# Ten RMS norms of a fused three-block kernel: sums put with tokens on partitions, the root taken on two columns, the result spread by TensorE

## The chip, the cores and the metric

The kernel runs on one NeuronCore of one Trainium2 chip. The metric is the device time of one execution in microseconds (us), taken as the median of several runs. A profiled execution beside them gives a trace of every instruction on the core: TensorE (PE, with its weight loads as PEld), VectorE (DVE), ScalarE (ACT), GpSimd (POOL), and the queue of SyncE (SP), which here issues all DMAs.

## What is computed

A batch of one, 256 tokens, width 1024, all float32. First a two-layer block (each layer: SwiGLU FFN, a mixer, SwiGLU FFN; the mixers are MLA and RWKV-7), then a second block (a Hyena and HGRN mixer, then 16 experts, each taking its 32 best tokens). Every stage begins with the same norm, modulated by vectors that come from a condition c:

```python
def _rmsnorm(x, g):
    y = x * rsqrt(mean(x * x, axis=-1, keepdims=True) + EPS)
    return y * g

def _modulate(x, g, shift, scale):
    return _rmsnorm(x, g) * (1 + scale) + shift

for i in range(2):
    mods = (silu(c) @ ada_w[i] + ada_b[i]).reshape(B, 3, 3, D_MODEL)
    h = _modulate(x, norm_g[i, 0], mods[:, 0, 0], mods[:, 0, 1])
    x = x + 0.5 * mods[:, 0, 2] * _swiglu(h, ffn_w_in[i, 0], ffn_w_out[i, 0])
    h = _modulate(x, norm_g[i, 1], mods[:, 1, 0], mods[:, 1, 1])
    x = x + mods[:, 1, 2] * mixer(h)          # MLA for i = 0, RWKV-7 for i = 1
    h = _modulate(x, norm_g[i, 2], mods[:, 2, 0], mods[:, 2, 1])
    x = x + 0.5 * mods[:, 2, 2] * _swiglu(h, ffn_w_in[i, 1], ffn_w_out[i, 1])
x = _rmsnorm(x, final_g)
# second block: norm, w_in, Hyena + HGRN, w_out, norm, router and experts, final norm
```

## The kernel before

Activations are held transposed: `x3` (tile `xT`) and `h3` (in `hT_sq`) have the 1024 features on partitions, as 8 tiles of 128 features (kt or m = 0 to 7), and the 256 tokens along the free dimension. Weights come from DRAM as slots of 1 or 2 MB. Each engine has its instruction stream written out by hand, in program order, and the engines meet at semaphores. There is no scheduler.

**A norm, before.** Norms are numbered 0 to 9. Norm 0 stands at the launch, norm 1 ahead of MLA, 2 and 3 ahead of FFNs 1 and 2, 4 ahead of RWKV, 5 ahead of FFN 3, 6 is the last norm of the first block, 7 and 8 are the first of the second block (of x, and of a context), 9 stands ahead of the router. ScalarE squares x in four steps of two tiles (L1386) into `sq3`. TensorE multiplies a 128x128 matrix of ones (the stationary operand) with each squared tile (256 columns, L664), so that PSUM bank 7 holds the sum of squares of each token, repeated on all 128 partitions. VectorE scales it and adds epsilon (L1728, 128x256), ScalarE takes the root (L1374, 128x256), VectorE the reciprocal (L1724, 128x256), all in the tile `rstd`. Then VectorE makes eight tiles of h, each `x * scale * rstd` (L1731), and ScalarE adds the shift to each (L1391), and TensorE's next stage waits for each of the eight in turn (`h_part`).

After the sums TensorE issues some matmuls on zeros (`keep_clock`, L659, bf16, 512 columns) whose result nobody reads. The number of them stands in the call: `norm(2, 10)` is norm 2 with 10 of them.

**The launch, before.** SP issues silu's input `c_rows`, one slot of the modulation weights (`ada`), then x, `vec` and a part of `con` (the `start_landed` loads), then two `ada` slots, the first FFN's gate and up slots, five `ada` slots, and the down slot. Then come four `ada` slots, each after a wait for a dot product of VectorE (`ada_used`), and the next gate slot once TensorE is done with the first. VectorE takes dot products of the `ada` slots with silu(c) (`first_dots`, L1757, two for each slot q = 0 to 7); slot q gives scale and shift for tile q of x. VectorE takes q = 0 and 1 ahead of norm 0 and q = 2 to 7 behind it. GpSimd multiplies x with `rstd` (L1688). ScalarE makes h (L1402 to L1408) when the dots and GpSimd's tile are there, and `first_group` on TensorE (L722) takes the eight tiles of h one by one.

**Between norm 6 and the second block.** TensorE computes the spectra of two filters, `filter_freq(0)` and `filter_freq(1)` (L1039 to L1043). The second may begin when VectorE has emptied the PSUM banks of the first (`filter_end(0)`, whose last instruction is L2083). Norm 7's sums stand between the two. In VectorE's stream norm 7's root and reciprocal follow `filter_end(0)`. Norm 8's sums stand between two units of `b2_in` (L1071), a chain of products of 7 us each, and its result is wanted three units later.

**The end.** The experts read 192 slots of 2 MB (`expert_load`, L597) into nine places of SBUF, each refilled when TensorE has used it. The ninth is issued behind the transposition of h after norm 9, and the tenth when TensorE has used the first.

## Time and profile before

| | us |
|---|---|
| median of 3 runs | 2678.49 |
| lowest, highest | 2677.92, 2680.62 |
| the profiled execution | 2676.36 |
| its span in the trace | 2674.30 |
| PE busy | 2302.1 (86%) |
| DVE busy | 774.6 (29%) |
| ACT busy | 344.9 (13%) |
| DMA queue q1 | 707.79 MB, 65.6% of 16 engines |

The span is what lies between the first and the last instruction; 2.06 us of the profiled execution lie around it. The busy shares are means over stages of different kinds: up to some 1750 us TensorE is the busy engine, after it the DMA engines are.

### The profile page before, as it was taken

Reading aid. Unit: us, or ns where it says so; the run is one execution under the profiler, and the core shown is the slowest. Engines: PE = TensorE matmul, PEld = TensorE weight load, DVE = VectorE, ACT = ScalarE, POOL = GpSimd, SP = SyncE. Lnnn points to the kernel's source line nnn. Section 1 sums busy time; section 2 is a strip of 40 time slices with the busy share of each in tenths; the row PEclk is TensorE's granted clock in tenths of the full one; section 3 lists DMA queues with packets and bytes.
Section 4 is the critical chain, followed back from the end, with each engine's and each line's share of the span. In section 5 each row is a group of like instructions: output and inputs, shape, how many; then the busy total and the mean of one; then the engine's idle time right before and its main releaser. Section 6 shows DMA issues by size and latency. Waiting matters only on the chain.

```text
span 2674.3 us, 34093 instructions
## 1 busy us (share of the span) xinstructions
PE 2302.1 (86%) x14956; PEld 1619.0 (61%) x14968; DVE 774.6 (29%) x1473; ACT 344.9 (13%) x618; POOL 17.5 (1%) x21
## 2 busy tenths in 40 slices
PE   7999989999999999999999999896666666666675
PEld 5888768888888789888886878652121111111221
DVE  5544534574000465511023338640000000000000
ACT  3001222002000232111002211210000000000000
POOL 1000000000000000000000000000000000000000
PEclk9999999999999999999999999988887788887778
DMA  9889235886445240044442223489999999999997
GB/s 394 343 354 379 95 142 226 354 341 256 157 141 204 90 147 20 24 169 148 136 172 78 66 77 115 189 330 428 428 427 428 426 428 427 428 427 427 426 428 338
DMA packets 70098, 709.51 MB, mean 265 GB/s; under 512 B 7776, under 2 KB 7904, under 8 KB 8672
## 3 DMA queue, kind: packets, MB, share of 16 engines
q1 hardware_dynamic: 69984, 707.79, 65.6%
q8 instruction: 96, 1.57, 0.2%
q14 instruction: 18, 0.15, 0.0%
HBM read 706.71 MB, written 1.05 MB: 265 GB/s over the span
## 4 chain that ended last, share of the span: by engine, by line
PE 62%; DMA 30%; DVE 7%; ACT 1%; issue 1%; SPq 0%; DVEq 0%; ACTq 0%
DMA arena<-in_experts 27%; PE ps L691 11%; PE ps L698 11%; PE ps L708 11%; PE ps L757 5%; PE ps L875 4%; PE ps L1071 4%; PE ps L1282 2%; PE ps L1314 2%; DMA ring<-in_experts 2%; PE ps L664 1%; PE ps L1069 1%; PE ps L773 1%; PE ps L1247 1%; PE ps L787 1%
## 5 line engine op out<-in xcount | busy, mean ns | idle before, releaser
L1282 PE MATMUL ps<-arena 128*32 128x512 f32 x1376 | 211.8, 748 | 147.0 <-DMA arena<-in_experts 146.5
L691 PE MATMUL ps<-hT_sq,arena 128*128 128x256 f32 x1376 | 312.1, 380 | 4.1 <-ACT hT_sq L1391 2.9
L708 PE MATMUL ps<-hid,arena 128*128 128x256 f32 x1408 | 311.1, 379 | 0.2 <-DVE hid L1796 0.2
L698 PE MATMUL ps<-hT_sq,arena 128*128 128x256 f32 x1376 | 311.0, 379 | 0.0
L708 PEld LDWEIGHTS ps<-hid,arena 128*128 128x128 f32 x1408 | 267.4, 190 | 36.9 <-issue 0.6
L691 PEld LDWEIGHTS ps<-hT_sq,arena 128*128 128x128 f32 x1376 | 260.5, 190 | 45.5 <-issue 8.5
L698 PEld LDWEIGHTS ps<-hT_sq,arena 128*128 128x128 f32 x1376 | 261.4, 190 | 35.5
L1282 PEld LDWEIGHTS ps<-arena 128*32 128x32 f32 x1376 | 42.4, 124 | 310.6 <-DMA arena<-in_experts 226.0
L1363 ACT ACTIVATE arena<-ps 128x512 f32<-128x512 f32 (+4 forms) x147 | 89.1, 615 | 946.1 <-PE ps L1293 308.5
L1796 DVE TENSOR_TENSOR hid<-sil,ps 128x256 f32<-128x256 f32 x88 | 37.0, 421 | 560.4 <-ACT sil L1415 560.2
L1757 DVE CUSTOM_DVE_ANT_0 hT_sq<-arena 128x1024 f32<-128x1024 f32 x168 | 194.5, 1221 | 0.0
L2249 DVE TENSOR_TENSOR arena<-arena,ps 128x512 f32<-128x512 f32 x16 | 11.0, 688 | 552.4 <-PE ps L1282 552.4
L1314 PE MATMUL ps<-arena 128*32 128x512 f32 x688 | 108.7, 767 | 36.5 <-DMA arena<-in_experts 33.1
L1415 ACT ACTIVATE sil<-ps 128x256 f32<-128x256 f32 x88 | 33.7, 383 | 779.3 <-PE ps L698 778.9
L1282 PE MATMUL ps<-ring,arena 128*32 128x512 f32 x512 | 79.3, 751 | 48.3 <-DMA ring<-in_experts 48.3
L757 PE MATMUL ps<-arena,ring 128*128 128x256 f32 x512 | 111.5, 379 | 2.6 <-DVE arena L1894 1.8
L757 PEld LDWEIGHTS ps<-arena,ring 128*128 128x128 f32 x512 | 97.1, 190 | 17.6 <-DVE arena L1894 2.3
L2256 DVE TENSOR_TENSOR arena<-ps,arena 128x512 f32<-128x512 f32 x16 | 11.1, 692 | 306.4 <-PE ps L1314 306.4
L875 PE MATMUL ps<-arena 64*64 64x64 f32 x2848 | 85.9, 218 | 3.0 <-ACT arena L1363 2.1
L875 PEld LDWEIGHTS ps<-arena 64*64 64x64 f32 x2848 | 84.4, 135 | 3.8 <-ACT arena L1363 2.5
L1314 PEld LDWEIGHTS ps<-arena 128*32 128x32 f32 x688 | 22.4, 128 | 105.7 <-DMA arena<-in_experts 49.0
L1071 PE MATMUL ps<-hT_sq,ring 128*128 128x256 f32 x384 | 83.9, 379 | 0.0
(370 smaller groups left out, 2184.0 us busy)
## 6 DMA issues: line engine op xcount, KB each, us to landing
arena<-in_experts SPq DMA_DIRECT2D x129, 2048.0 KB, 41.1
arena<-in_ada SPq DMA_DIRECT2D x96, 1024.0 KB, 9.7
ring<-in_experts SPq DMA_DIRECT2D x42, 2048.0 KB, 40.9
ring<-in_ring_w SPq DMA_DIRECT2D x51, 1024.0 KB, 5.1
arena<-in_ffn_gate SPq DMA_DIRECT2D x44, 1024.0 KB, 6.5
arena<-in_ffn_up SPq DMA_DIRECT2D x44, 1024.0 KB, 6.2
arena<-in_ffn_down SPq DMA_DIRECT2D x44, 1024.0 KB, 4.8
hT_sq<-in_experts SPq DMA_DIRECT2D x21, 2048.0 KB, 40.4
```

The source lines that it names most:

```text
L691: last = mm(ps[:, ft, 0:T], gate3[:, kt, ft * P:(ft + 1) * P], h3[:, kt, :], start=kt == 0, stop=kt == KT - 1)
L698: last = mm(ps[:, ft, T:2 * T], up3[:, kt, ft * P:(ft + 1) * P], h3[:, kt, :], start=kt == 0, stop=kt == KT - 1)
L708: last = mm(acc(m), down3[:, ft, m * P:(m + 1) * P], hid3[:, ft, :], start=False, stop=True, skip_group_check=True)
L757: last = mm(out_of(m), slot(seq0 + kt // 2)[:, (kt % 2) * D + m * P:(kt % 2) * D + (m + 1) * P], rhs3[:, kt, :], start=(kt == 0 and m % 2 ...
L875: last = mm(ps[r, bank, kt * HD:(kt + 1) * HD], lhs[r, kt, :], rhs[r, :] if len(rhs.shape) == 2 else rhs[r, kt, :], start=start and (stop ...
L1071: last = mm(o, w[:, kt, j * P:(j + 1) * P], src[:, kt, :], start=kt == 0, stop=kt == KT - 1)
L1282: last = mm(ps[32 * n:32 * n + 32, part, :], e_xe[:, kt, :], w[:, (kt % 2) * SLOT + n * 512:(kt % 2) * SLOT + (n + 1) * 512], start=kt == ...
L1314: last = mm(ps[q:q + 32, 3, :], e_hT[:, i, 32 * n:32 * n + 32], w[:, i * D + nn * 512:i * D + (nn + 1) * 512], start=n == 0 and i < 2, sto ...
L1363: return f(dst, src, ACT.Copy)
L1415: f(sil3[:, ft, :], ps[:, ft, 0:T], ACT.Silu).then_inc(sem("silu_ready"), 1)
L1757: nc.vector.tensor_tensor_reduce(buf[:, out_at * D:(out_at + 1) * D], w, c_rows[:, which * D:(which + 1) * D], 1.0, 0.0, ALU.mult, ALU.add ...
L1796: tt_(hid3[:, ft, :], sil3[:, ft, :], ps[:, ft, T:2 * T], ALU.mult).then_inc(sem("hid_ready"), 1)
```

## The change

- **Sums.** The squared tile becomes the stationary operand, in two halves of 128 tokens, and one column of ones the moving one: 16 matmuls of one column in place of 8 of 256. The sums of the two token halves stand in two PSUM columns, `norm_sums`, with tokens on partitions.
- **Root and reciprocal** work on 128x2 (`norm_unit`, in `small`).
- **Spreading.** `widen` multiplies each column of `norm_unit`, repeated 128 times by its access pattern as the stationary operand, with the identity: two matmuls of 128x128 into `norm_wide`, half of PSUM bank 7. VectorE reads that in place of `rstd`. In TensorE's stream `widen` stands behind 5 or 6 matmuls on zeros and waits for the reciprocal. In norm 7 it stands ahead of `filter_freq(1)`, in norm 8 behind one more unit of `b2_in`.
- **The launch.** x, `vec` and `con` are loaded first. ScalarE squares x before silu. VectorE takes only q = 0 ahead of norm 0, multiplies x with the spread root itself, and takes q = 1 to 7 behind that. GpSimd has no part in it. TensorE has 16 more matmuls on zeros ahead of the sums.

```diff
-        def norm_sums(i):
-            return ps[:, 7, 0:T]
+        norm_sums, norm_wide, norm_unit = ps[:, 7, 0:TT], ps[:, 7, T:2 * T], small[:, 240:240 + TT]
...
+            start()
             sp.dma_start(c_rows[:, 0:D], a["c_rows"][:, 0:D]).then_inc(sem("c_landed"), 16)
-            first_rows(0, 1)
-            start()
-            first_rows(1, 3)
+            first_rows(0, 3)
...
-            def norm(i, busy=0):
+            def norm(i, busy=(0, 0)):
+                if i == 7:
+                    pe.wait_ge(sem("x_ready"), 7 * KT)
                 for kt in range(KT):
                     pe.wait_ge(sem("squares"), 4 * i + kt // 2 + 1)
-                    last = mm(norm_sums(i), ones, sq3[:, kt, :], start=kt == 0, stop=kt == KT - 1)
+                    for tt in range(TT):
+                        last = mm(norm_sums[:, tt:tt + 1], sq3[:, kt, tt * P:(tt + 1) * P], ones[:, 0:1],
+                                  start=kt == 0 and tt == 0, stop=kt == KT - 1, skip_group_check=True)
                 last.then_inc(sem("norm_sum"), 1)
-                keep_clock(6, busy)
+                if busy:
+                    keep_clock(6, busy[0])
+                    widen(i)
+                    keep_clock(6, busy[1])
+
+            def widen(i):
+                pe.wait_ge(sem("norm_unit"), i + 1)
+                for tt in range(TT):
+                    last = mm(norm_wide[:, tt * P:(tt + 1) * P], norm_unit[:, tt:tt + 1].to_broadcast([P, P]), ident,
+                              start=True, stop=True)
+                last.then_inc(sem("norm_wide"), 1)
...
-                        norm(8)
+                        norm(8, None)
+                    if u == CTX_AT + 1:
+                        widen(8)
...
+            keep_clock(6, 16)
             pe.wait_ge(sem("start_landed"), 48)
-            norm(0, 12)
+            norm(0, (6, 20))
             ffn(0, 1)
-            norm(1, 20)
+            norm(1, (5, 8))
             mla()
-            norm(2, 10)
+            norm(2, (5, 2))
             ffn(1, 3)
-            norm(3, 10)
+            norm(3, (5, 2))
             ffn(2, 4)
-            norm(4, 18)
+            norm(4, (5, 9))
             rwkv()
-            norm(5, 10)
+            norm(5, (5, 2))
             ffn(3, 6)
-            norm(6, 11)
+            norm(6, (5, 5))
             filter_freq(0)
-            norm(7)
+            norm(7, None)
+            keep_clock(0, 5)
+            widen(7)
             filter_freq(1)
...
-            norm(9, 10)
+            norm(9, (5, 3))
...
-                root(rstd[:, :])
+                if i == 0:
+                    act.wait_ge(sem("c_landed"), 16)
+                    f(c_rows[:, 0:D], c_rows[:, 0:D], ACT.Silu).then_inc(sem("c_ready"), 1)
+                root(norm_unit)
...
-            act.wait_ge(sem("c_landed"), 16)
-            f(c_rows[:, 0:D], c_rows[:, 0:D], ACT.Silu).then_inc(sem("c_ready"), 1)
...
-            pool.wait_ge(sem("x_root"), 1)
-            for kt in range(KT):
-                nc.gpsimd.tensor_tensor(x_unit[:, kt, :], x3[:, kt, :], rstd[:, :], ALU.mult).then_inc(sem("x_scaled"), 1)
...
-                inverse_root(ts(rstd[:, :], norm_sums(i), 1.0 / D, EPS, ALU.mult, ALU.add), rstd[:, :])
+                root(ts(norm_unit, norm_sums, 1.0 / D, EPS, ALU.mult, ALU.add))
+                nc.vector.reciprocal(norm_unit, norm_unit).then_inc(sem("norm_unit"), 1)
+                dve.wait_ge(sem("norm_wide"), i + 1)
                 for m in range(KT):
-                    stt(out=dst[:, m, :], in0=src[:, m, :], scalar=scale[:, m:m + 1], in1=rstd[:, :], op0=ALU.mult, op1=ALU.mult) \
+                    stt(out=dst[:, m, :], in0=src[:, m, :], scalar=scale[:, m:m + 1], in1=norm_wide, op0=ALU.mult, op1=ALU.mult) \
                         .then_inc(sem(name), 1)
...
-            first_dots(0, 2)
+            first_dots(0, 1)
...
-            root(ts(rstd[:, :], norm_sums(0), 1.0 / D, EPS, ALU.mult, ALU.add))
-            nc.vector.reciprocal(rstd[:, :], rstd[:, :]).then_inc(sem("x_root"), 1)
-            first_dots(2, 2 * NADA)
+            root(ts(norm_unit, norm_sums, 1.0 / D, EPS, ALU.mult, ALU.add))
+            nc.vector.reciprocal(norm_unit, norm_unit).then_inc(sem("norm_unit"), 1)
+            dve.wait_ge(sem("norm_wide"), 1)
+            for kt in range(KT):
+                tt_(x_unit[:, kt, :], x3[:, kt, :], norm_wide, ALU.mult).then_inc(sem("x_scaled"), 1)
+            first_dots(1, 2 * NADA)
```

In the lists below a row is a run of equal instructions of one engine in program order; `x8` counts them, and a float32 matmul counts once here though the trace shows two records for it.

TensorE around norm 2, before: L664 are the sums, L659 the matmuls on zeros, L675 opens the banks of FFN 1, L691 is its first product.

```order
L757 MATMUL ps<-hT_sq,ring 128x256 x64
L664 MATMUL ps<-hT_sq,con 128x256 x8
L659 MATMUL ps<-zeros 128x512 x10
L675 MATMUL ps<-zeros 128x512 x4
L736 UNCONDITIONAL_BRANCH
L736 ISA
L691 MATMUL ps<-hT_sq,arena 128x256 x8
```

The same place after the change: L664 are the sums, L656 the matmuls on zeros, L676 is `widen`, L687 opens the banks.

```order
L769 MATMUL ps<-hT_sq,ring 128x256 x64
L664 MATMUL ps<-con,hT_sq 128x1 x16
L656 MATMUL ps<-zeros 128x512 x5
L676 MATMUL ps<-con,small 128x128 x2
L656 MATMUL ps<-zeros 128x512 x2
L687 MATMUL ps<-zeros 128x512 x4
L748 UNCONDITIONAL_BRANCH
L748 ISA
L703 MATMUL ps<-hT_sq,arena 128x256 x8
```

The ten matmuls on zeros have become five, `widen`, and two.

TensorE around norm 7, before: L664 are norm 7's sums, the first L1039 below them begins `filter_freq(1)`.

```order
L1043 MATMUL ps<-arena 128x512 x2
L664 MATMUL ps<-hT_sq,con 128x256 [waits squares] x8
L1039 MATMUL ps<-arena 128x512 [waits filter_done,filter_sides]
L1039 MATMUL ps<-arena 128x512
L1041 MATMUL ps<-arena 128x512 x2
```

The end of the sums of norm 7 and what follows, after the change: L1051 begins `filter_freq(1)`.

```order
L664 MATMUL ps<-con,hT_sq 128x1 [waits squares]
L664 MATMUL ps<-con,hT_sq 128x1
L656 MATMUL ps<-zeros 128x512 x5
L676 MATMUL ps<-con,small 128x128 [waits norm_unit]
L676 MATMUL ps<-con,small 128x128
L1051 MATMUL ps<-arena 128x512 [waits filter_done,filter_sides]
L1051 MATMUL ps<-arena 128x512
L1053 MATMUL ps<-arena 128x512 x2
```

`filter_freq(1)` now stands behind a wait for norm 7's reciprocal (`norm_unit`) as well, and behind `widen`.

VectorE at the launch, before: L1757 are the dot products of q = 1, then norm 0 (L2286, L2287), then q = 2. A row `dots 128x1` belongs to the dot product above it.

```order
L1757 ISA arena,dots<-arena 128x1024 [waits ada_first,ada_landed1]
L1757 ISA dots 128x1
L1757 ISA arena,dots<-arena 128x1024 [waits ada_used]
L1757 ISA dots 128x1
L2283 SCALAR_TENSOR_TENSOR coef<-vec 128x8 [waits start_landed]
L2286 TENSOR_SCALAR rstd<-ps 128x256 [waits norm_sum]
L2287 RECIPROCAL rstd<-rstd 128x256 [waits root_out]
L1757 ISA arena,dots<-arena 128x1024 [waits ada_first,ada_landed2]
```

The same place after the change: norm 0 is L2302 and L2303, the eight multiplications of x are L2306, and q = 1 follows.

```order
L1773 ISA arena,dots<-arena 128x1024
L1773 ISA dots 128x1
L2299 SCALAR_TENSOR_TENSOR coef<-vec 128x8 [waits start_landed]
L2302 TENSOR_SCALAR small<-ps 128x2 [waits norm_sum]
L2303 RECIPROCAL small<-small 128x2 [waits root_out]
L2306 TENSOR_TENSOR arena<-xT,ps 128x256 [waits norm_wide]
L2306 TENSOR_TENSOR arena<-xT,ps 128x256 x7
L1773 ISA arena,dots<-arena 128x1024 [waits ada_first,ada_landed1]
```

The dot products of q = 1 to 7 now stand behind the multiplications of x.

## Rows read from the trace of the kernel before

**Rows 1.** Page: DMA share in 40 slices (tenths); the chain by engine

```profile
DMA  9889235886445240044442223489999999999997
...
PE 62%; DMA 30%; DVE 7%; ACT 1%; issue 1%; SPq 0%; DVEq 0%; ACTq 0%
```

**Rows 2.** Timeline, norm 2: start us, us, engine, line, operation [idle before <-releaser]

```profile
403.67 3.62 PE L664 MATMUL ps<-hT_sq,con 128*128 128x256 f32 x16
...
404.79 0.63 ACT L1386 ACTIVATE hT_sq<-xT 128x512 f32<-128x512 f32 x1 [0.24 <-DVE xT L1752]
...
407.34 2.10 PE L659 MATMUL ps<-zeros 128*128 128x512 bf16 x9
407.40 0.42 DVE L1728 TENSOR_SCALAR rstd<-ps 128x256 f32<-128x256 f32 x1 [2.58 <-PE ps L664]
407.86 0.42 ACT L1374 ACTIVATE rstd<-rstd 128x256 f32<-128x256 f32 x1 [1.14 <-DVE rstd L1728]
408.31 1.75 DVE L1724 RECIPROCAL rstd<-rstd 128x256 f32<-128x256 f32 x1 [0.48 <-ACT rstd L1374]
...
410.10 3.25 DVE L1731 SCALAR_TENSOR_TENSOR hT_sq<-xT,coef,rstd 128x256 f32<-128x256 f32 x8
...
411.27 3.04 PE L691 MATMUL ps<-hT_sq,arena 128*128 128x256 f32 x13 [0.95 <-ACT hT_sq L1391]
```

**Rows 3.** Timeline around 1594 us: another root and reciprocal, on 128x2

```profile
1594.84 0.20 ACT L1374 ACTIVATE small<-small 128x2 f32<-128x2 f32 x1
1595.07 0.17 DVE L1724 RECIPROCAL small<-small 128x2 f32<-128x2 f32 x1 [1.34 <-ACT small L1374]
```

**Rows 4.** Timeline of TensorE, 1745 to 1794 us: float32 matmuls, stationary 128x128

```profile
1745.23 7.03 PE L1247 MATMUL ps<-arena 128*128 128x32 f32 x32
...
1782.40 3.74 PE L1302 MATMUL ps<-con,xT 128*128 128x128 f32 x32
...
1789.64 3.76 PE L1247 MATMUL ps<-arena 128*128 128x32 f32 x32
```

**Rows 5.** Timeline: the last two dot products at launch, FFN 0's second group

```profile
36.62 0.08 DVE L1757 DVE_READ_ACCUMULATOR2_ANT dots<- 128x1 f32 x1
...
37.76 0.08 DVE L1757 DVE_READ_ACCUMULATOR2_ANT dots<- 128x1 f32 x1
...
49.84 3.72 PE L691 MATMUL ps<-hT_sq,arena 128*128 128x256 f32 x16 [1.25 <-DMA arena<-in_ffn_gate]
```

**Rows 6.** Stretches: us, PE, PEld, DVE, ACT, POOL busy, PEclk, DMA share, GB/s

```profile
20.00:36.00 16.00, 12.14 (x46) 9.85 (x47) 15.24 (x21) 6.65 (x18) 12.16 (x8) 0.89 1.01 420
36.00:50.00 14.00, 11.90 (x52) 9.22 (x51) 10.62 (x19) 5.26 (x9) 0.00 (x0) 1.00 1.02 413
```

**Rows 7.** The launch's last two `ada` slots: issues, and issue to landing

```profile
L561 SPq DMA_DIRECT2D arena<-in_ada x2: 458/612/765, 7.1 to 7.6; - x2
...
DMA to landing us min/median/max: 23.7/24.7/25.7
```

**Rows 8.** Timeline of TensorE: the first product of MLA, after norm 1

```profile
267.38 22.64 PE L773 MATMUL ps<-hT_sq,ring 128*128 128x256 f32 x96 [2.31 <-ACT hT_sq L1391]
```

**Rows 9.** Two of the slots it reads (1 and 2): issue and landing

```profile
L592 SPq DMA_DIRECT2D ring<-in_ring_w x2: 447/450/454, 241.8 to 242.3; - x2
...
DMA to landing us min/median/max: 22.9/23.8/24.8
```

**Rows 10.** Timeline of norm 7 and the begin of `filter_freq(1)`

```profile
1427.67 1.22 DVE L2083 TENSOR_TENSOR arena<-ps,arena 128x1024 f32<-128x1024 f32 x1
1428.80 0.41 DVE L1728 TENSOR_SCALAR rstd<-ps 128x256 f32<-128x256 f32 x1
...
1429.03 3.34 PE L1039 MATMUL ps<-arena 128*128 128x512 f32 x4 [4.01 <-DVE arena L2083]
```

**Rows 11.** A stretch of it, columns as in rows 6

```profile
1429.00:1432.00 3.00, 2.97 (x4) 1.42 (x5) 2.48 (x4) 0.42 (x1) 0.00 (x0) 0.53 0.02 5
```

**Rows 12.** Timeline of TensorE behind norm 8's sums

```profile
1471.63 20.88 PE L1071 MATMUL ps<-hT_sq,ring 128*128 128x256 f32 x96
```

## The prediction

> **What bounds the kernel now.** I read the page first: the chain that ended last lies on TensorE for 62% of the span and on DMA for 30%, on VectorE for 7% [rows 1]. The slices of DMA show where each holds: nearly full in the first four slices (267 us), partly full up to slice 27, full from there to the end [rows 1]. So up to some 1750 us a microsecond saved on TensorE's path ahead of a stage is a microsecond of the whole, and the experts' DMA stream behind it starts as much earlier: its tenth slot is asked for when TensorE has used the first. What it takes from then on does not depend on the norms. Two places differ: where TensorE, when a norm is done, waits for a transfer all the same, and where TensorE does not wait for the norm at all. So I took the ten norms one by one, each with the timeline around it, and asked which wait of TensorE ends last there.
>
> The profiled execution took 2676.36 us, of which 2674.30 are the span. The sum is made against it. The median of the runs is 2.13 us above it, and the forecast is the median plus the sum.
>
> **A norm on the path.** Norm 2 stands for norms 2, 3, 4, 5 and 9, which look alike. TensorE begins the sums at 403.67 and VectorE the first tile of h at 410.10 [rows 2]: 6.43 us. Of these the sums are 3.62, then 0.11 to VectorE, 0.42 scaling, 0.04, 0.42 root, 0.03, 1.75 reciprocal, 0.04.
>
> After the change the sums are 16 float32 matmuls of one column, 32 records. No row shows one column. The nearest show 32 columns with a 128x128 stationary operand: 32 records in 3.76 us, and the same with 128 columns in 3.74 [rows 4]. Since four times the columns cost no more, it is the load of the stationary operand that sets the pace, 0.117 us a record, and one column should cost that too: 3.75 us in place of 3.62. At the slower clock level the same 32 took 7.03, or 0.22 each [rows 4], and that is the upper bound. The lower bound is that the sums end with the last square, at 405.42 in place of 407.29 [rows 2], 1.9 us less.
>
> The Trainium skill says in "TensorE: Matmul & The Clock Gate" (section LDWEIGHTS) that a load takes its number of columns over 1.2 GHz, 107 ns for 128, whatever the moving side has. The same page's table of issue gaps (Back-to-back issue gap) allows a matmul of 1 to 64 columns every 25 ns. By the first the sums cost as I take them, by the second they would hide behind the squares. The 0.117 of the row speaks for the first.
>
> Then 0.11 to VectorE, 0.17 for scaling 128x2 (I take the reciprocal's time on that shape), 0.04, root 0.20, 0.03, reciprocal 0.17 [rows 3]: the unit column is there 4.47 us after the begin. From VectorE's end to TensorE's start I take 0.14 (1428.89 to 1429.03 [rows 10]), so `widen` could begin at 4.61. But five matmuls on zeros stand ahead of it, at (2.10 - 0.38) / 8 = 0.215 each [rows 2], 0.38 being the last one's own tail as in the sums, and TensorE gets there at 3.7 + 1.08 = 4.76. `widen` is 4 records of 128 columns, 0.45 and a tail of 0.16, end 5.37, and VectorE starts at 5.48. That is 0.95 less than 6.43; without rounding TensorE's part up it is 1.04. I take 1.0 for each of the five, **-5.0**. VectorE's read of PSUM in place of SBUF costs nothing here: its tiles come every 0.41 us, and TensorE takes 0.43 for the two records of each. Behind `widen` stand two matmuls on zeros and four that open banks, 1.3 us, and the first tile of h comes 1.17 after VectorE's start (411.27 less 410.10 [rows 2]), 6.65 against TensorE's 6.5: not in the way.
>
> **Norm 1: 0.** TensorE begins MLA at 267.38, though ScalarE's first tile was ready earlier; the profile names ScalarE, but slot 2, issued at 242.3, took 24.8 to land: 267.1 [rows 8, 9]. That is the wait that ends last. These loads are issued by events of FFN 0, so norm 1's microsecond only lengthens the idle time, from 2.3 to 3.3.
>
> **The launch.** Slots q = 6 and 7 land at 30.8 and 33.3 [rows 7]. The bytes ahead of them are the same after the change, only their order differs. Before, VectorE ended its last dot at 37.84, at 1.14 us a dot [rows 5], because two pairs stood behind a late start. After, x lands first; squares, silu, one more table load, q = 0, the root and eight products are done at about 19 us by my estimate, and from q = 4 on VectorE is there before the slots. The last pair then ends at 33.4 + 2.3 = 35.7, and h's last tile comes 2.1 earlier. FFN 0's first group ends 2.1 earlier too. But TensorE's second group starts at 49.84 behind a wait of 1.25 for the gate slot [rows 5], and the DMA engines are full all the way: share 1.01 and 1.02 in the stretches ahead [rows 6]. The gate slot is asked for earlier, behind the same bytes, and lands when it did. So the 2.1 become idle time: 3.35 in place of 1.25. **0**, and a price on top:
>
> **The clock.** In the trace TensorE's granted clock fell to its lower level (1.2 of 2.4 GHz) behind the idle time of 4.0 us in norm 7 (0.53 over the 3 us that follow) [rows 10, 11], behind the 2.3 of norm 1, and once between 20 and 36 us (0.89) [rows 6]. After 0.95 and 1.25 us the 13 and 16 records that follow ran at the full pace [rows 2, 5]. Behind norm 1 the 96 records took 22.64, where 96 at the full clock took 20.88 [rows 8, 12]: a fall costs 1.76. The new idle of 3.35 at 46.5 will likely have one, **+1.75**. Behind norm 1 there was one already.
>
> **Norm 6: +0.45.** TensorE does not wait for its result: `filter_freq(0)` needs the residual only. So TensorE pays the sums' pace, 32 x 0.115 against 16 x 0.216 (20.88 / 96 = 0.2175 with its tail), +0.2, and 10 zeros and `widen` (2.15 + 0.45) in place of 11 (2.37), +0.25.
>
> **Norm 7: +1.0.** Here the change adds a wait. Queued behind it on TensorE is `filter_freq(1)`, and behind that the whole of `b2_in`. It began at 1429.03, 0.14 behind VectorE's last instruction of `filter_end(0)` [rows 10]. Now it must wait for the root as well: 1428.80 + 0.17 + 0.04 + 0.20 + 0.03 + 0.17 + 0.14 = 1429.55, and 0.45 of `widen`: 1430.0. VectorE and ScalarE finish h sooner, but nobody waits for that; `filter_freq(1)` takes longer. The idle of 4.0 becomes 3.4, since the five matmuls on zeros fill some. If the clock then stays up, the four matmuls of 3.34 [rows 10] would save up to 1.5; I leave it as it was.
>
> **Norm 8: +0.7.** Sums +0.25, `widen` +0.45, in a chain where TensorE does not stop (96 records in 20.88 [rows 12]). VectorE waits a unit longer, with nothing due behind it, and ScalarE's emptying of a bank comes some 4 us later, which the unit of 7 us on the other bank covers.
>
> **Sum:** -5.0 + 1.75 + 0.45 + 1.0 + 0.7 = -1.1. Forecast 2678.49 - 1.1 = **2677.4 us**.
>
> **Rivals.**
> - *No new fall of the clock, the rest as above:* -1.1 - 1.75 = -2.85, **2675.6**. The idle time of 2.3 in norm 1 speaks against it. If the falls at norms 1 and 7 go as well (-1.76, -1.5), 2672.4.
> - *The launch's gain gets through:* the gate slot lands 2.1 earlier, no idle, no fall: -1.1 - 2.1 - 1.75 = -4.95, **2673.5**. For it speaks that the slot and its last forerunner are asked for 2 us sooner; against it that no stretch ahead of it shows room.
> - *One-column sums hide behind the squares:* 1.7 us more on norms 2 to 6, 8 and 9, -12: **2665.5**. Rows 4 speak against.
> - *Slower:* loading squares as the stationary operand is slower than the 0.117 of rows 4. At 0.19 us a record the 32 take 6.1 in place of 3.7, 2.4 more on the same seven norms, +16.8 and **2694**. It decides from where 7 x 32 x the excess is over 5.4 + 1.1 us: an excess of 0.029, a pace of 0.145. For it speaks the 0.22 of rows 4, if the clock is down; against, that it was up in every norm but the first.
>
> **How the numbers follow.** A measurement of this kernel tells 0.2%, 5.4 us, from no change. Forecast 0.42, no new fall 0.25 (a fifth of it with the other falls gone), launch's gain through 0.14 (a third of it beyond 0.2%), hidden sums 0.04, slower sums 0.06. The last 0.09 is for the clock ahead of the first expert slots, which may fall otherwise by a few us either way. Faster 0.17, same 0.76, slower 0.07. The range leaves out hidden and slower sums and reaches to the case with all falls gone: 2672 to 2681.
>
> **What would show it.** Right: `widen` 4.6 to 4.8 us behind the begin of the sums of norms 2 to 5 and 9, h's first tile 1.0 earlier, 32 records of sums in 3.7; the second group of FFN 0 still at 49.8 with an idle time near 3.3 and the clock down behind it; MLA's first product at the same distance from its slot's landing; `filter_freq(1)` 1.0 later against `filter_end(0)`. Wrong: if the sums' pace is not 0.115 to 0.12, if the gate slot lands at 48 or earlier, or if TensorE meets a bank not yet emptied behind norm 8.

## The result: slower by 0.45%

The kernel before took 2678.2 us (median of 6 runs, 2674.0 to 2680.6), the changed one 2690.2 us (6 runs, 2685.6 to 2692.9). The ratio is 1.0045, with an interval from 1.0033 to 1.0057. The forecast was 2677.4 us, in a range of 2672 to 2681. The changed kernel lies outside it, on the slow side.

The profiled execution of the changed kernel took 2691.3 us, its span 2689.5 us (2674.3 before). Two views show where the 15.2 us are. First the stretches of TensorE, of the kernel before and then of the changed one. The columns are: stretch, its length, TensorE's busy time and records, granted clock, share of the DMA engines, GB/s.

```profile
core 0 of [0], span 2674.3 us
...
250.00:300.00 50.00, 44.24 (x193) 0.97 0.53 217
300.00:415.00 115.00, 104.71 (x534) 1.00 0.27 107
415.00:650.00 235.00, 233.99 (x1083) 1.00 0.83 326
650.00:890.00 240.00, 238.12 (x1103) 1.00 0.43 149
890.00:1170.00 280.00, 272.43 (x4553) 1.00 0.21 73
1170.00:1425.00 255.00, 254.95 (x1119) 1.00 0.44 157
1425.00:1500.00 75.00, 69.78 (x297) 0.98 0.29 99
```

```profile
core 0 of [0], span 2689.5 us
...
250.00:300.00 50.00, 46.36 (x208) 0.90 0.56 228
300.00:415.00 115.00, 105.48 (x543) 0.97 0.26 101
415.00:650.00 235.00, 234.92 (x1099) 0.99 0.82 326
650.00:890.00 240.00, 239.15 (x1119) 0.99 0.42 149
890.00:1170.00 280.00, 271.94 (x4554) 0.99 0.21 73
1170.00:1425.00 255.00, 254.92 (x1139) 0.99 0.44 157
1425.00:1500.00 75.00, 70.43 (x301) 0.89 0.25 84
```

TensorE's mean granted clock is lower in every stretch that holds a norm. What is called a fall below is a stretch of time in which the granted clock was at its lower level. Counted from the trace's record of the granted clock, all falls ahead of norm 9's first product add up to 61 us, where they were 20 us before.

The second view is the timeline of norm 2 after the change, which answers to [rows 2]:

```profile
403.09 4.27 PE L664 MATMUL ps<-con,hT_sq 128*128 128x1 f32 x32
...
407.47 0.16 DVE L1742 TENSOR_SCALAR small<-ps 128x2 f32<-128x2 f32 x1 [3.23 <-PE ps L664]
407.60 1.91 PE L656 MATMUL ps<-zeros 128*128 128x512 bf16 x4 [0.24 <-issue]
407.66 0.20 ACT L1391 ACTIVATE small<-small 128x2 f32<-128x2 f32 x1 [1.53 <-DVE small L1742]
407.90 0.17 DVE L1743 RECIPROCAL small<-small 128x2 f32<-128x2 f32 x1 [0.27 <-ACT small L1391]
409.31 1.06 PE L676 MATMUL ps<-con,small 128*128 128x128 f32 x4
410.16 1.06 PE L656 MATMUL ps<-zeros 128*128 128x512 bf16 x2
410.41 3.22 DVE L1747 SCALAR_TENSOR_TENSOR hT_sq<-xT,coef,ps 128x256 f32<-128x256 f32 x8 [2.35 <-PE ps L676]
...
411.02 1.87 PE L687 MATMUL ps<-zeros 128*128 128x512 bf16 x4
412.72 1.46 PE L703 MATMUL ps<-hT_sq,arena 128*128 128x256 f32 x6
```

The unit column is ready at 408.07, 4.98 us behind the first sum. But TensorE still works through zeros, at 0.43 us each and not 0.215, and begins `widen` at 409.31. `widen`, two more zeros and `open_banks` run at half pace as well, so FFN 1's first product comes 9.63 us behind the first sum, where 7.60 were needed before. What was 0.95 us of waiting on ScalarE is now TensorE being late itself.

The same reading for each norm, from the first sum to the next first product, in us:

| norm | before | after | run 1 (wide sums) |
|---|---|---|---|
| 2 | 7.60 | 9.63 | 6.46 |
| 3 | 7.60 | 7.98 | 6.46 |
| 4 | 9.33 | 9.48 | 8.19 |
| 5 | 7.60 | 9.61 | 6.46 |
| 6 | 5.83 | 7.77 | 6.17 |
| 7 | 7.63 | 9.05 | 8.58 |
| 8 (sums only) | 3.56 | 5.82 | 3.68 |
| 9 | 7.50 | 7.52 | 6.67 |

After the change norms 2 to 7 lose 7.9 us, and norm 8 with the 32 products and the `widen` behind it 5.5. RWKV, whose code is unchanged, took 1.65 us more, all of it in its later part: from its first product to the first record of line 887 (line 875 before) it took 119.4 us in both. Kernels without any fall in RWKV differ by more than that (last section), so the 1.65 is not shown to come from the change. A fall of the clock that stood in the HGRN part before was shorter, which gave back 1.5. With -0.6 up to norm 2 and small differences elsewhere, norm 9's first product comes 12.5 us later (1744.25 for 1731.74). Behind it the experts took 945.3 us for 942.6; in all kernels below it was 942.5 to 946.1, whatever was changed ahead of it. So 2.7 us of the 15.2 lie within what single traces differ by there. The medians differ by 12.0.

### The profile page after: what moved, and what is told of

Read it like the earlier page. It is cut to its first block, busy times and chain, and to the rows that moved or that the text cites. A ratio compares the mean times of both kernels' runs of the same rounds, so it can differ in the third digit from the quotient of the medians.

```text
span 2689.5 us, 34515 instructions
## 1 busy us (share of the span) xinstructions
PE 2335.8 (87%) x15166; PEld 1649.1 (61%) x15180; DVE 755.2 (28%) x1481; ACT 344.0 (13%) x619; POOL 5.2 (0%) x13
## 4 chain that ended last, share of the span: by engine, by line
PE 63%; DMA 30%; DVE 6%; ACT 1%; issue 1%; SPq 0%; DVEq 0%; ACTq 0%
DMA ring<-in_experts 20%; PE ps L703 11%; PE ps L720 11%; PE ps L710 11%; DMA arena<-in_experts 8%; PE ps L769 5%; PE ps L1085 4%; PE ps L887 4%; PE ps L1296 2%; PE ps L1328 2%; PE ps L664 1%; PE ps L1083 1%; DMA arena<-in_ada 1%; PE ps L1261 1%; PE ps L799 1%; PE ps L785 1%
## 5 line engine op out<-in xcount | busy, mean ns | idle before, releaser
L1296 PE MATMUL ps<-arena 128*32 128x512 f32 x1376 | 219.4, 773 | 136.3 <-DMA arena<-in_experts 135.7
L1328 PE MATMUL ps<-arena 128*32 128x512 f32 x688 | 112.7, 793 | 34.4 <-DMA arena<-in_experts 29.6
L1085 PE MATMUL ps<-hT_sq,ring 128*128 128x256 f32 x384 | 86.9, 388 | 0.0
```

The costliest lines, as they stand in the source:

```text
L1085: last = mm(o, w[:, kt, j * P:(j + 1) * P], src[:, kt, :], start=kt == 0, stop=kt == KT - 1)
L1296: last = mm(ps[32 * n:32 * n + 32, part, :], e_xe[:, kt, :], w[:, (kt % 2) * SLOT + n * 512:(kt % 2) * SLOT + (n + 1) * 512], start=kt == ...
L1328: last = mm(ps[q:q + 32, 3, :], e_hT[:, i, 32 * n:32 * n + 32], w[:, i * D + nn * 512:i * D + (nn + 1) * 512], start=n == 0 and i < 2, sto ...
```

## The experiments

Runs are called by the number in their label (there is no result with number 2). A norm's sums are 16 float32 matmuls in the new form, which leave 32 records; some expectations call the records matmuls. Run 1's expectation counts 34 us at the lower clock for the kernel before: 13.7 of them lie behind norm 9's first product. Each run has one trace, so where falls stood is known for one execution of each; the medians are of 4 to 11 executions. Times are medians, the interval is that of the ratio to the kernel before.

| run | us | ratio | interval |
|---|---|---|---|
| e1 wide sums | 2677.6 | 0.9998 | 0.9989 to 1.0007 |
| e3 no zeros ahead | 2695.9 | 1.0064 | 1.0049 to 1.0079 |
| e4 launch alone | 2679.7 | 1.0010 | 1.0000 to 1.0019 |
| e5 24 idle in before | 2704.4 | 1.0088 | 1.0071 to 1.0105 |
| e6 wide in norm 8 alone | 2682.8 | 1.0017 | 1.0008 to 1.0027 |
| e7 wide, launch of before | 2673.1 | 0.9982 | 0.9973 to 0.9991 |
| e8 wide, norms 6 to 8 of before | 2673.5 | 0.9983 | 0.9974 to 0.9992 |
| e9 12 idle in before | 2679.2 | 1.0001 | 0.9992 to 1.0011 |
| e10 12 wide in before | 2678.0 | 0.9998 | 0.9989 to 1.0008 |
| e11 e7 and e8 together | 2673.9 | 0.9984 | 0.9975 to 0.9993 |
| e12 e1 with cover | 2675.0 | 0.9994 | 0.9985 to 1.0003 |
| e13 16 idle in before | 2685.7 | 1.0029 | 1.0020 to 1.0039 |
| e14 e8 with cover | 2672.7 | 0.9978 | 0.9969 to 0.9987 |
| e15 every other sum wide | 2677.4 | 1.0005 | 0.9993 to 1.0016 |

### Columns or way: runs 1 and 3

```
-last = mm(norm_sums[:, tt:tt + 1], sq3[:, kt, tt * P:(tt + 1) * P], ones[:, 0:1],
+last = mm(norm_sum_wide[:, tt * P:(tt + 1) * P], sq3[:, kt, tt * P:(tt + 1) * P], ones,
...
+norm_sums = ps[:, 7, 0:T:P]
```

> The changed kernel with one thing put back: each of the 32 sum matmuls of a norm streams 128 columns of ones again and not one (the same squares are loaded as the stationary side, the same sums come out, 128 times over, and VectorE reads one column of each half). Theory A, the clock: the stream of one-column matmuls is what lets TensorE's granted clock fall to its lower level in nearly every norm of the changed kernel (61 us at the lower level ahead of the experts, against 34 in the kernel before). The falls at norms 1 to 6 and 8 then go, with at most 35 us at the lower level ahead of the experts; from the first sum of norm 2 to the next layer's first product it takes 6.6 to 6.8 us (7.60 before, 9.63 in the changed kernel), since the sums themselves last as long (32 x 0.117 = 3.74 us, by the pace of the 32 records of 128 columns in the stage of the experts) and the prediction's 1.0 us for the small root comes through; 2671 to 2676 us in all. Theory B, the serial way: the loss is the way itself (five zero matmuls, then the widening, then two more groups in front of the next product), whatever the clock. Then nothing changes: 9 to 10 us at norm 2 and 2689 to 2691 us.

Run 3's edit is in `norm`:

```
-keep_clock(6, busy[0])
+zeros_ahead = 0 if 2 <= i else busy[0]
+keep_clock(6, zeros_ahead)
 widen(i)
-keep_clock(6, busy[1])
+keep_clock(6, busy[1] + busy[0] - zeros_ahead)
```

> The changed kernel, with the five zero matmuls that stand between the sums and the widening of norms 2 to 6 and 9 put behind the widening. The column sums, the loads and all else stay. Theory A (the clock): the sums still let the clock fall, 55 us or more at the lower level ahead of the experts; what is won is only the time by which zeros at the lower clock (4 x 0.43 = 1.7 us in norms 2 and 5) run past the reciprocal (ready 0.6 us behind the last sum), at most 1.1 us a norm; 2684 to 2691 us. Theory B (the zeros in front of the widening are what makes the new way longer): from the first sum to the next first product 7.5 us or less at norms 2, 3 and 5, and 2678 us or less in all.

Run 1, norm 2, timeline of TensorE and VectorE, and then the stretches around it, of the changed kernel and of run 1:

```profile
404.88 3.73 PE L665 MATMUL ps<-con,hT_sq 128*128 128x128 f32 x32
...
408.45 1.24 PE L657 MATMUL ps<-zeros 128*128 128x512 bf16 x5
...
409.53 0.61 PE L677 MATMUL ps<-con,small 128*128 128x128 f32 x4
...
410.17 3.22 DVE L1748 SCALAR_TENSOR_TENSOR hT_sq<-xT,coef,ps 128x256 f32<-128x256 f32 x8 [0.86 <-PE ps L677]
410.40 1.03 PE L688 MATMUL ps<-zeros 128*128 128x512 bf16 x4
...
411.34 2.83 PE L704 MATMUL ps<-hT_sq,arena 128*128 128x256 f32 x12
```

```profile
403.00:406.00 3.00, 3.00 (x29) 0.98 0.00 0
406.00:409.00 3.00, 2.76 (x11) 0.50 0.00 0
409.00:412.00 3.00, 3.00 (x11) 0.50 0.00 0
```

```profile
403.00:406.00 3.00, 3.00 (x21) 1.00 0.00 0
406.00:409.00 3.00, 3.00 (x27) 1.00 0.00 0
409.00:412.00 3.00, 3.00 (x17) 1.00 0.00 0
```

The same loads, the same order and the same waits, with 128 columns in place of one: the sums take 3.73 us, the falls at norms 2 to 8 are gone, and norm 2 takes 6.46 us. The whole is 12.6 us faster than the changed kernel. Theory A holds, but its 2671 to 2676 us for the whole did not come; a fall in FFN 0 explains up to 1.7 us of that (below, launch and late norms). Theory B falls with run 1, and again with run 3. There `widen` began 4.87 us behind the first sum of norm 3, where the changed kernel needed 5.12, and yet norms 2, 3 and 5 took 8.91, 10.20 and 8.86 us and the whole 2695.9, beyond what A had expected too: TensorE then waits between sums and `widen`, and the clock was down for 70 us ahead of norm 9's first product. The zeros stood there with reason.

### One norm: run 6

```
-last = mm(norm_sums[:, tt:tt + 1], sq3[:, kt, tt * P:(tt + 1) * P], ones[:, 0:1],
+out_, cols = (ps[:, 7, tt * P:(tt + 1) * P], P) if i == 8 else (ps[:, 7, tt:tt + 1], 1)
+last = mm(out_, sq3[:, kt, tt * P:(tt + 1) * P], ones[:, 0:cols],
```

> The changed kernel with 128 columns of ones in the sums of norm 8 alone, one column in all others. In the changed kernel the clock fell for 10.2 us from the start of norm 8's sums: the sums took 5.97 us (3.63 at full clock) and the 32 products behind them 9.89 us (7.07), 5.2 us more than at full clock. Theory A (the clock falls behind the stream of one-column matmuls that is under way, each norm for itself): this fall goes and no other changes; the sums of norm 8 take 3.7 to 3.8 us, the 32 products 7.1, and the time is 5.2 us less, 2684 to 2687 us. Rival (the falls come from the whole of what the core does, and one taken away comes elsewhere soon after): norm 8 recovers but the time stays at 2689 or more.

First the changed kernel, then run 6, TensorE at norm 8 (run 6's line 679 are the sums, of which the first eight records stand further up; L1085 and L1100 are the same products):

```profile
1476.53 5.97 PE L664 MATMUL ps<-con,hT_sq 128*128 128x1 f32 x32 [1.20 <-ACT hT_sq L1403]
1482.35 9.89 PE L1085 MATMUL ps<-hT_sq,ring 128*128 128x256 f32 x32
```

```profile
1473.81 2.84 PE L679 MATMUL ps<-con,hT_sq 128*128 128x128 f32 x24
1476.49 7.07 PE L1100 MATMUL ps<-hT_sq,ring 128*128 128x256 f32 x32
```

Norm 8 recovers as A says, by 5.0 us. The falls ahead of norm 9's first product add up to 44 us for 61, so norm 8's 10.2 did not come elsewhere as a whole, though norm 7's fall was 10.2 us long for 6.8. The time is 7.4 us less, though, and not 5.2: other norms, which this run did not change, lost less than in the changed kernel's profile (norm 2 took 7.98 us, norm 5 6.37). Falls at one norm differ between kernels with the same norm.

### One-column matmuls in the kernel before: runs 5, 9, 10 and 13

Behind the last sum of norms 1 to 5 of the kernel before, in the place of zeros (n is 24, 12, 12 and 16, and run 13 has 16 for both 12s of the last changed line; run 10 has `ones[:, 0:P]` and `ps[:, 6, 0:P]`):

```
 last.then_inc(sem("norm_sum"), 1)
+if 1 <= i <= 5:
+    for j in range(n):
+        mm(ps[:, 6, 0:1], ident, ones[:, 0:1], start=True, stop=True)
+    busy -= 12 if busy > 12 else busy
 keep_clock(6, busy)
```

> The kernel before, with nothing of the change in it but 24 one-column float32 matmuls on loaded constants (the identity as the stationary side, one column of ones through it) behind the sums of norms 1 to 5, in the place of zero matmuls: of all ten behind the sums of norms 2, 3 and 5, and of twelve of them in norms 1 and 4. At full clock 24 x 0.113 = 2.7 us stand where 2.1 us of zeros and 0.95 us of waiting stood, so they hold nothing up by themselves. Nobody reads their result. Theory A (the clock): the granted clock falls now at norms 2, 3 and 5, where it stayed up in the kernel before, for 3.4 or 6.8 us each, and the time rises by half of what TensorE works through at the lower level, 1.7 to 3.4 us a fall: 2681 to 2688 us. Theory B (the loss of the changed kernel is its serial way through the widening): no new fall, 2677 to 2680 us.

Run 5 said less than it was meant to: its 24 matmuls left 48 records, which take 5.4 us at full clock and hold norm 2 up by themselves. It showed falls at all five norms and 2704.4 us.

> Run 5 again with half the matmuls. Its trace showed 48 records for the 24 one-column float32 matmuls, two each, so that they took 5.4 us even at full clock and not 2.7: they held norm 2 up by about 2.3 us of their own, and the clock's part could not be told from that. Here 12 one-column matmuls (24 records x 0.113 = 2.7 us) stand behind the sums of norms 1 to 5 of the kernel before, where 2.1 us of zeros and 0.95 us of waiting stood in norms 2, 3 and 5. At full clock the next product is not later. Theory A (a stream of one-column matmuls lets the clock fall): falls of 3.4 or 6.8 us at norms 2, 3, 4 and 5, where the kernel before has none, sums to next product 8.5 us or more (7.60 before), 2682 to 2687 us. Rival (one-column matmuls are harmless, and run 5 lost its time by length alone): 7.6 to 7.7 us at norms 2, 3, 5, no fall, 2677 to 2680 us.

> The control to run 9: the same 12 float32 matmuls at the same places, with 128 columns through each and not one (24 records x 0.117 = 2.8 us). Theory A: no new fall of the clock, 7.6 to 7.8 us from the sums to the next product at norms 2, 3 and 5, and 2677 to 2680 us, as the kernel before. Rival (float32 weights loaded one behind the other bring the fall, however many columns follow each): the same falls and the same time as run 9.

> Between runs 9 and 5: the kernel before with 16 one-column matmuls (32 records, as many as a norm's sums of the changed kernel have) behind the sums of norms 1 to 5, in the place of ten zero matmuls (norms 2, 3, 5) or sixteen (norms 1, 4). At full clock 32 x 0.113 = 3.6 us stand where 3.05 us of zeros and waiting stood, so norms 2, 3 and 5 take about 8.2 us (7.60 before) and the whole 2 us more for it: 2680 us. Run 9 (24 records) fell at norm 2 alone, run 5 (48 records) at every norm. Theory A (a stretch of one-column matmuls as long as that of the changed kernel's sums brings the falls, by itself): falls at three or more of norms 1 to 5, 9 us or more from sums to next product where they are, 2684 to 2692 us. Rival (it takes something else of the changed kernel as well, the widening or the way to it): a fall at norm 2 at most, 2679 to 2682 us.

The stretches around norms 2, 4 and 5, of runs 10, 9 and 13 in this order:

```profile
403.00:420.00 17.00, 16.51 (x88) 1.00 0.00 0
...
875.00:900.00 25.00, 23.20 (x119) 1.00 0.16 48
1155.00:1190.00 35.00, 34.51 (x172) 1.00 0.32 114
```

```profile
403.00:420.00 17.00, 16.57 (x83) 0.90 0.00 0
...
875.00:900.00 25.00, 23.09 (x118) 1.00 0.13 43
1155.00:1190.00 35.00, 34.40 (x171) 1.00 0.27 90
```

```profile
403.00:420.00 17.00, 17.00 (x89) 0.90 0.00 0
...
875.00:900.00 25.00, 23.20 (x110) 0.86 0.10 31
1155.00:1190.00 35.00, 35.00 (x172) 0.95 0.18 60
```

The control to run 9, run 10, is the kernel before in time and clock at these norms. Run 9 had one fall at norm 2, and its time is that of the kernel before: the 2682 to 2687 us that A gave were wrong. Run 13, with as many one-column records as the changed kernel's sums, fell at norms 2, 4 and 5 and lost 7.5 us, of which at most 2 are the longer stretch itself. At norms 2 and 5 TensorE was not idle at all (17.00 of 17 and 35.00 of 35 us busy), while run 10 had short waits there and no fall. So one-column matmuls in the number of the changed kernel do it by themselves, with no `widen` beside them, and fewer mostly do not. No run has 16 wide matmuls in this place: that the 16 loads of run 13 are not the cause rests on run 1, whose sums are 16 wide matmuls a norm. In run 13 norm 3 kept its clock. Most of the falls lies behind the next first product, and the sum-to-product times (8.22, 7.80, 9.34, 7.81) hardly show them; the stage behind does. From norm 4's product to the first record of line 879 in RWKV it took 122.4 us, where the same way (to line 875) took 119.4 before, and 119.3 to 119.4 in every other kernel but run 5. The 3.0 us are the fall's. RWKV as a whole took 274.7 us for 270.1; the other 1.6 came later in it, where kernels without a fall differ as much.

### Their number in the changed kernel: run 15

```
-last = mm(norm_sums[:, tt:tt + 1], sq3[:, kt, tt * P:(tt + 1) * P], ones[:, 0:1],
+out_, cols = (ps[:, 7, P:2 * P], P) if tt == 1 else (ps[:, 7, 0:1], 1)
+last = mm(out_, sq3[:, kt, tt * P:(tt + 1) * P], ones[:, 0:cols],
```

> The changed kernel with 128 columns of ones in every other sum matmul (those of the second 128 tokens) and one column in the rest: the same 32 records and loads in each norm, 3.7 us. Theory A (what counts is how much of the stretch streams nothing): 8 one-column matmuls a norm, spread over it, are fewer than the 12 of run 9, which brought one fall in five norms; then the falls at norms 2 to 6 and 8 mostly go, norms 2, 3 and 5 take 6.5 us, and the time is 2676 to 2681 us. Rival (a one-column matmul after each wide one does the same harm as a run of them): falls at most norms, 2686 us or more.

The stretches around norms 2, 4 and 5 of run 15:

```profile
403.00:420.00 17.00, 17.00 (x97) 1.00 0.00 1
875.00:900.00 25.00, 24.01 (x118) 1.00 0.25 85
1155.00:1190.00 35.00, 35.00 (x172) 1.00 0.43 160
```

Norms 2 to 6 took 6.46, 6.46, 8.19, 6.46 and 6.17 us, just as in run 1, with the clock up from norm 2 to norm 6 (the same stretches as above for runs 9, 10 and 13). Norm 8 had a fall (sums 5.42 us, 3.84 in run 1). Theory A holds for norms 2 to 6 and for the time, and the rival falls; norm 8 shows that the half-wide form is no sure cure.

### Launch and late norms: runs 4, 7, 8, 11, 12 and 14

Run 4 is the changed kernel with norms 1 to 9 as before. Run 7 is the kernel before, launch included, with wide sums and `widen` in norms 1 to 9. Run 8 is run 1 with norms 6 to 8 as before. Run 11 is run 7 with norms 6 to 8 as before. Runs 12 and 14 are runs 1 and 8 with this in `first_group`:

```
 second_half(0)
+keep_clock(6, 8)
```

> The launch part of the change alone: x loaded first, the Silu behind the squares, norm 0 in the new form and x scaled on VectorE, while norms 1 to 9 stand as in the kernel before (256-column sums with ones as the stationary side, root and reciprocal over 256 columns). Theory A (the clock, set off by one-column sums in norms 1 to 9): no loss is left, 2676.5 to 2678.5 us, norm 2 at 7.6 us and the clock up at norms 2 to 6; the second group of FFN 0 starts at 49.5 as in the changed kernel. Rival C (the launch part itself costs, by a later stream of weights or the clock behind it): 2680 us or more, and the second group of FFN 0 or norm 1 stands later than in the kernel before.

> The kernel before with the new form, 128 columns wide, in norms 1 to 9, and its launch as it was (Silu first, 256-column sums, root and reciprocal over 256 columns, GpSimd scales x). Run 1 (all norms wide, new launch) showed norms 2 to 5 shorter by 1.14 us each, norm 1 by 0.37 and norm 9 by 0.83, norms 6, 7 and 8 longer by 0.34, 0.95 and 0.12, which is 4.35 us less, and norm 1 begun 1.58 us later than before, behind a fall of the clock at the second group of FFN 0. Theory L (the new launch costs what the prediction put at 1.75 us for that fall): without it the first product behind norm 9 stands 4.0 to 4.7 us earlier than in the kernel before (at 1727.0 to 1727.8), and the time is 2673.5 to 2675.5 us. Rival R (what is won ahead of the experts is given back there, where the experts' stream of DMA and its clock set the end): the first product stands as early, and the time is 2676.5 to 2678.5 us all the same.

> As run 1 (128 columns, new launch), but norms 6, 7 and 8 in the form of the kernel before, where the widening stood in front of work that the full-width root did not delay. Norm 6 takes 5.83 us again (6.17 in run 1), norm 7 7.63 (8.58), norm 8 3.56 (3.68): 1.41 us less than run 1 up to norm 9, unless the fall of the clock behind norm 7, which run 1 did not have (3.4 us at half clock, 1.7 us lost in the frequency products), comes back; then 0.3 us more. 2676 to 2677.5 us by the first, 2677.5 to 2679 by the second. By rival R, 2677 to 2678 in either case.

> The new form, 128 columns wide, where it paid in run 1 (norms 1 to 5 and 9); norms 6, 7 and 8 and the launch as in the kernel before. From run 7 (2673.0 us against 2678.7) it differs by norms 6 to 8 alone, in which the form of before is shorter by 0.34, 0.95 and 0.12 us; the 3.4 us fall behind norm 7, which run 7 did not have and run 8 had, comes back and takes up to 1.7 us. 2671.5 to 2674 us. Theory L (the new launch costs time): it lies below run 8 (2673.5), from which it differs by the launch alone, by 1 us or more. Rival (the launch is worth nothing either way, and runs 1 and 7 differ by chance): it lies within 1 us of run 8.

> Run 1 (all norms 128 columns wide, new launch; 2677.6 us) with 8 zero matmuls more, behind the first group of FFN 0 and ahead of its wait for the second group's gate slot (1.85 us idle there in the changed kernel, 3 us or more in run 1's trace together with its fall of the clock for 3.4 us). 8 x 0.22 = 1.75 us of zeros fit the wait. Theory L (run 1 lost to run 7 by the clock's fall in the second group's wait): no fall there, the start of norm 1's sums 1.7 us earlier than in run 1 (257.0 and not 258.7), and 2673 to 2676 us. Rival (the launch costs something else, or the fall comes elsewhere): norm 1 at 258.5 or later, or the clock falls elsewhere ahead of norm 2, and 2676.5 to 2678.5 us.

> Run 8 (new launch, 128 columns in norms 1 to 5 and 9, norms 6 to 8 as before; 2673.5 us) with the cover of run 12 (8 zero matmuls in the wait for the second group of FFN 0). If the fall in that wait comes in some of run 8's executions, the median falls by up to 1.7 us: 2671.5 to 2673.5 us. Rival (the cover is worth nothing where the fall does not come): 2673.5, the same as run 8 within 1 us.

Run 4's 2679.7 us lie between the two expectations, so it decides neither by its time.

TensorE at the second group of FFN 0 in the changed kernel, in run 1 and in run 12:

```profile
49.52 3.72 PE L703 MATMUL ps<-hT_sq,arena 128*128 128x256 f32 x16 [1.85 <-DMA arena<-in_ffn_gate]
```

```profile
49.73 5.41 PE L704 MATMUL ps<-hT_sq,arena 128*128 128x256 f32 x16 [1.86 <-DMA arena<-in_ffn_gate]
```

```profile
47.84 1.67 PE L663 MATMUL ps<-zeros 128*128 128x512 bf16 x7
49.65 3.72 PE L718 MATMUL ps<-hT_sq,arena 128*128 128x256 f32 x16
```

The same wait brought a fall in run 1 and none in the changed kernel. In run 1 it put norm 1's sums at 258.72; in all others they stand at 256.6 to 257.1. Run 12 had no fall ahead of norm 7, and its norm 1 began at 256.95, as theory L had it. Its median is 2.5 us below run 1's, but the two intervals overlap over most of their length, so the times do not show the gain.

Run 7's first product behind norm 9 came at 1724.46, 7.3 us before that of the kernel before. That is 2.6 more than expected, since the falls behind norms 1 and 7 were absent too, and 5.6 us of it are in the median; rival R falls. Run 8 came below its range. Run 11, expected below run 8, came at the same time, so the rival holds there. Four kernels (7, 8, 11, 14) gave 2672.7 to 2673.9 and are not told apart by their intervals: either launch with norms 6 to 8 as before, and the launch of before with them wide. The fourth pair, the new launch with norms 6 to 8 wide, gave 2677.6 (run 1) and 2675.0 (run 12, with the cover). Run 14's 0.8 us against run 8 is no more than its rival allows.

What the launch part is worth stays open. New against old launch with equal norms: +1.9 us (run 4 against before), +4.5 (run 1 against 7), -0.4 (8 against 11), and with the cover +2.0 (12 against 7) and -1.2 (14 against 11). Run 4's own trace shows the norms at 7.60 and one fall more than before, in MLA, behind a wait of 1.99 us on ScalarE that the kernel before has as well. Seven of the 16 kernels fell there, of either launch.

The lowest median is run 14's, 2672.7 us and 0.9978: 0.2% below the kernel before.

## Why the prediction was wrong

**What bounds the kernel.** Right. What norms 2 to 8 lost on TensorE's path reached norm 9, and the experts began later by that.

**A norm on the path (-5.0).** The working was right for a full clock. One-column sums took 3.63 us where the clock stayed up (3.75 forecast) and the 128-column sums of run 1 3.73. In run 1 `widen` began 4.65 us behind the first sum (4.76) and h's first tile came 5.29 behind it, 1.14 us earlier than before (1.0). The step that failed is the overlooked effect of the one-column form on the clock, a term that the sum has at nothing for norms 2 to 9. The prediction took one column to cost what 32 and 128 cost, because the load sets the pace; that holds for the sum itself and says nothing of what the engine has streamed meanwhile. It treated the clock as something that only waiting lowers: the paragraph on the clock names idle times alone, and the signs of being wrong name no clock behind a norm's sums. In the changed kernel TensorE was busy for 3.00 of 3 us from 403 to 406 and had 0.24 us without work behind that, and the clock was at its lower level over the next 6 us.

In its place the runs showed that with 128 columns, everything else being equal, the falls at norms 2 to 8 go and 12.6 us with them (run 1), and that 16 one-column matmuls a norm bring falls into the kernel before (run 13). Why the granted clock falls behind such a stream is not shown.

The sums themselves paid little. They were busy 41.5 us in all, 37.4 in run 1. The zeros, `widen`, `open_banks` and first products behind them paid the rest. For this reason the slower rival was no help: it looked for a slow load, which the runs did not show, with a time (2694) that lies near by accident. [Rows 4] had a weak hint that was read only as a pace. The clock had fallen at 1742.5, behind waits and 2.7 us ahead of the stream of 32-column records, but it stayed down through all 7.03 us of that stream, in which TensorE was busy.

The Trainium skill, in "TensorE: Matmul & The Clock Gate" (section HAM oscillation — how this bites in real kernels), ties a clock that falls again to waits between groups of matmuls. Here runs 1 and 15 took the falls of norms 2 to 6 away with the same waits in the program. Its section LDWEIGHTS, which the prediction weighed, gives 107 ns for 128 columns; the records took 0.113 us with one moving column and 0.117 with 128 at full clock, 6 to 9% above it. (3.7 + 1.08 in that part of the working is 4.78 and not 4.76, which changes nothing.)

**Norm 1 (0).** Right for the start of MLA: 266.8 to 267.4 in all kernels but runs 1 and 5. The idle time of 3.3 us did not come, since zeros, partly at half clock, filled it.

**Launch (0 and +1.75).** The gate slot did set the second group's start, 49.52 for 49.84. But the chain ended 0.9 us earlier and not 2.1, so TensorE waited 1.85 us and not 3.35. The fall did not come in the changed kernel's profile; it came in run 1's, where the 16 records took 1.69 us longer: right in size, wrong in being taken as likely each time.

**Norms 6, 7, 8 (+0.45, +1.0, +0.7).** In run 1: +0.34, +0.95, and 0.12 of sums with 0.44 of `widen`. In the changed kernel +1.94, +1.42 and +5.5, by the clock.

**The sum.** Forecast 2677.4, run 1 2677.6. The sum described the kernel with 128 columns; the missing term is the clock, 12.6 us, and slower had been given 0.07. That the two agree within 0.2 us is in part luck. In run 1's trace norm 9's first product came 2.7 us earlier than before, not 1.1, since the fall at norm 7 was gone, which the sum had left as it was; the experts took 1.2 us more, and the run's executions lie between 2674.6 and 2680.5.

## To carry to other kernels

Count what a new form of matmul streams through TensorE, not only how long it takes: a norm's worth of one-column matmuls behind one another can cost more in the stage behind them than they save. Where loads of 128 columns set the pace, a moving side of up to 128 columns costs next to nothing (3.73 us for 3.63 here), so widen it into spare PSUM and read one column. When a kernel keeps TensorE's clock up by hand, read the granted clock of every stretch that a change touches, and take a term for it into the sum with both signs.

## What the runs showed of the chip

- TensorE's granted clock fell with TensorE busy: run 10 and run 13 differ in the columns (and by 4 matmuls a norm), and only run 13 fell behind norms 2, 4 and 5, at norms 2 and 5 without any idle time of TensorE.
- At the lower level the zeros took 0.43 us each (0.215 at the full one), and `widen` 1.06 us (0.61 in run 1).
- The same wait brings a fall in some kernels and none in others: 1.86 us in FFN 0 (run 1, not the changed kernel), 1.99 us in MLA (7 of 16).
- A float32 matmul left two records, with one column or 128, so a pace per record is half of that per matmul.
- A fall can come behind the stretch that brought it: in run 13 it stood in RWKV.
- RWKV, unchanged in all kernels, took 270.1 us before and 271.8 in the changed kernel, and 270.9 to 273.4 in runs 1, 7, 8 and 14, with no fall in any of them. Differences of up to 3 us between single traces there mean nothing. The runs do not show what makes them.
